# Feed-forward products of a 256-token, thirteen-stage network on one Trainium2 core: three moving products of 256 columns in place of one of 512 and one of 256

## The reference, cut to what matters

```python
def swiglu(x, w_in, w_out):
    gate, up = jnp.split(x @ w_in, 2, axis=-1)
    return (jax.nn.silu(gate) * up) @ w_out
...
x = x + 0.5 * swiglu(rms(x, gain), w_in, w_out)   # w_in: 1024 x 5632, w_out: 2816 x 1024
```

## Time and profile before

| what | value |
|---|---|
| median of 3 executions | 2190.56 us (2188.40 to 2193.27) |
| the profiled execution | 2188.89 us |
| its span, first to last instruction | 2187.1 us |
| granted TensorE clock, mean over the span | 0.996 |
| matmuls | 14203 |

### The profile page before, as it was taken

How to read it: one execution, slowest core, us unless ns; L and a number is a source line. 1 busy time by engine, 2 the same in 40 slices (tenths; PEclk the granted TensorE clock), 3 DMA queues, 4 the chain that set the end, 5 groups by cost and what they waited for, 6 DMA issues and landing times.

```text
span 2187.1 us, 39606 instructions
## 1 busy us (share of the span) xinstructions
PE 2141.0 (98%) x14203; PEld 1930.5 (88%) x14203; DVE 1600.6 (73%) x1903; ACT 1301.1 (59%) x1801; POOL 583.3 (27%) x450
## 2 busy tenths in 40 slices
PE   8999899999999999999999999999999999999998
PEld 7889888888888899999888888999888888888887
DVE  7875798886787676666887687654887688677874
ACT  5664776665665556665665466454665466456663
POOL 3421662441342000000342143000342144122430
PEclk9999999999999999999999999999999999999999
DMA  6665457665566555544566566544566556534662
GB/s 211 193 201 168 126 176 259 191 203 184 172 191 213 167 164 159 159 147 149 173 192 204 166 193 218 161 137 144 173 192 209 164 190 195 189 109 145 192 218 99
DMA packets 371157, 387.92 MB, mean 177 GB/s; under 512 B 11334, under 2 KB 366031, under 8 KB 371056
## 3 DMA queue, kind: packets, MB, share of 16 engines
q1 hardware_dynamic: 357104, 369.14, 53.7%
q10 hardware_dynamic: 13952, 17.41, 2.5%
HBM read 376.02 MB, written 10.49 MB: 177 GB/s over the span
## 4 chain that ended last, share of the span: by engine, by line
PE 87%; DVE 7%; ACT 4%; issue 1%; POOL 0%; DMA 0%; ACTq 0%; DVEq 0%
PE ps L818 43%; PE ps L819 23%; PE ps L772 3%; PE ps L773 3%; PE ps L774 3%; DVE wlo L1683 1%; DVE xg L1701 1%; PE ps L862 1%; ACT whi L1275 1%; PE ps L793 1%; PE ps L794 1%; PE ps L795 1%; PE ps L863 1%; PE ps L864 1%; PE ps L1003 1%
## 5 line engine op out<-in xcount | busy, mean ns | idle before, releaser
L1683 DVE TENSOR_TENSOR wlo<-raw,whi 128x1024 fp32r<-128x1024 f32 (+2 forms) x652 | 881.7, 1363 | 155.0 <-ACT whi L1275 154.0
L818 PE MATMUL ps<-xg,whi 128*128 128x512 f32 x2816 | 981.9, 392 | 3.7 <-DVE xg L1701 1.7
L1275 ACT ACTIVATE whi<-raw 128x1024 fp32r<-128x1024 f32 (+2 forms) x652 | 720.7, 1113 | 192.4 <-PE ps L819 130.4
L819 PE MATMUL ps<-xg,wlo 128*128 128x256 f32 x2816 | 794.6, 282 | 0.0
L818 PEld LDWEIGHTS ps<-xg,whi 128*128 128x128 f32 x2816 | 529.4, 188 | 117.9 <-DVE xg L1701 3.5
L819 PEld LDWEIGHTS ps<-xg,wlo 128*128 128x128 f32 x2816 | 532.9, 189 | 0.2
L818 PE MATMUL ps<-hT,whi 128*128 128x512 f32 x1408 | 488.5, 390 | 0.0
L819 PE MATMUL ps<-hT,wlo 128*128 128x256 f32 x1408 | 397.1, 282 | 0.0
L818 PEld LDWEIGHTS ps<-hT,whi 128*128 128x128 f32 x1408 | 264.3, 188 | 55.4
L819 PEld LDWEIGHTS ps<-hT,wlo 128*128 128x128 f32 x1408 | 266.1, 189 | 0.0
L2183 POOL TENSOR_TENSOR gate_r<-gate,r 128x512 f32<-128x512 f32 x88 | 189.6, 2154 | 286.7 <-DVE gate L1761 286.7
(11 more groups left out here) (276 smaller groups left out, 3003.3 us busy)
## 6 DMA issues: line engine op xcount, KB each, us to landing
raw<-in_ffn_w_in SPq DMA_DIRECT2D x352, 512.0 KB, 3.5
raw<-in_ffn_w_out SPq DMA_DIRECT2D x64, 768.0 KB, 4.8
raw<-in_ffn_w_out SPq DMA_DIRECT2D x64, 640.0 KB, 4.9
raw<-in_w_kv SPq DMA_DIRECT2D x48, 512.0 KB, 3.6
raw<-in_a_w_in SPq DMA_DIRECT2D x32, 512.0 KB, 4.2
raw<-in_b_w_q SPq DMA_DIRECT2D x24, 512.0 KB, 3.9
raw<-in_sb_w_qkv SPq DMA_DIRECT2D x24, 512.0 KB, 4.4
bias_by_distance<-bias_rows ACTq DMA_DIRECT2D x12, 768.0 KB, 5.4
```

The costliest lines, as they stand in the source:

```text
L818: nc.tensor.matmul(out, whi[:, par, w], both, start=first and k == 0, stop=False)
L819: mm = nc.tensor.matmul(out[:, 0:T], wlo[:, par, w], both[:, 0:T], start=False, stop=last and k == total - 1)
L1275: nc.scalar.activation(whi[:, par, off:off + size], raw[:, 2 * par + half, :size], ACT.Copy).then_inc(hi_done, 1)
L1683: nc.vector.tensor_tensor(wlo[:, par, off:off + size], raw[:, 2 * par + half, :size], whi[:, par, off:off + size].bitcast(F32), ALU.subtra ...
```

## The change

`wide_products` becomes `ffn_products`. For each chunk and half it issues three matmuls of 256 columns, all into the same 256 columns of one bank: half m of the slot is columns 256m to 256m+255. `start` is set on the slot's first matmul alone. The up slots use banks 4 and 0, the down slots banks 3 and 5. In "up" ACT's copy takes the whole sum (512 columns of one bank) and raises `evac_done` itself; the DVE additions of lines 1756 and 1768 are gone, with their semaphores. In "down" one DVE instruction in place of two adds half of the sum to `x`.

```diff
-    UP_BANKS, DOWN_BANKS = (3, 0), (3, 5)
+    UP_BANKS, DOWN_BANKS = (4, 0), (3, 5)
...
-                    both = moving[:, chunk0 + k, :, :].rearrange("p s t -> p (s t)")
+                    hi, lo = moving[:, chunk0 + k, 0, :], moving[:, chunk0 + k, 1, :]
                     for m in range(2):
-                        out = ps[:, bank + m, :]
+                        out = ps[:, bank, T * m:T * (m + 1)]
                         w = slice(W2 * k + P * m, W2 * k + P * (m + 1))
-                        nc.tensor.matmul(out, whi[:, par, w], both, start=first and k == 0, stop=False)
-                        mm = nc.tensor.matmul(out[:, 0:T], wlo[:, par, w], both[:, 0:T], start=False, stop=last and k == total - 1)
+                        nc.tensor.matmul(out, whi[:, par, w], hi, start=first and k == 0 and m == 0, stop=False)
+                        nc.tensor.matmul(out, whi[:, par, w], lo, start=False, stop=False)
+                        mm = nc.tensor.matmul(out, wlo[:, par, w], hi, start=False, stop=last and k == total - 1 and m == 1)
...
-                nc.scalar.activation(pair(gate[:, :]), wide(UP_BANKS[0], 0), ACT.Copy).then_inc(gate_copied, 1)
+                nc.scalar.activation(gate[:, :], ps[:, UP_BANKS[0], :], ACT.Copy).then_inc(evac_done, 1)
...
-                nc.scalar.activation(pair(h[:, :]), wide(UP_BANKS[1], 0), ACT.Copy).then_inc(h_copied, 1)
+                nc.scalar.activation(h[:, :], ps[:, UP_BANKS[1], :], ACT.Copy).then_inc(evac_done, 1)
...
-                dve.wait_ge(gate_copied, p + 1)
-                nc.vector.tensor_tensor(pair(gate[:, :]), wide(UP_BANKS[0], 1), pair(gate[:, :]), ALU.add).then_inc(evac_done, 1)
...
-                dve.wait_ge(h_copied, p + 1)
-                nc.vector.tensor_tensor(pair(h[:, :]), wide(UP_BANKS[1], 1), pair(h[:, :]), ALU.add).then_inc(evac_done, 1)
...
-                nc.vector.scalar_tensor_tensor(pair(xpair(m)), wide(DOWN_BANKS[m % 2], 1), 0.5, pair(xpair(m)), ALU.mult, ALU.add).then_inc(half_added, 1)
-                dve.wait_ge(half_added, NPAIR * f + m + 1)
-                nc.vector.scalar_tensor_tensor(pair(xpair(m)), wide(DOWN_BANKS[m % 2], 0), 0.5, pair(xpair(m)), ALU.mult, ALU.add).then_inc(evac_done, 1)
+                nc.vector.scalar_tensor_tensor(xpair(m), ps[:, DOWN_BANKS[m % 2], :], 0.5, xpair(m), ALU.mult, ALU.add).then_inc(evac_done, 1)
```

More of the change, by code:

```diff
@@ L343, in build_program @@
     r_col_ready = sem("r_col_ready")
-    gate_copied = sem("gate_copied")
-    h_copied, h_made = sem("h_copied"), sem("h_made")
+    h_made = sem("h_made")
     gate_made = sem("gate_made")
-    half_added = sem("half_added")
     gate_exp = sem("gate_exp")
@@ L393, in hidden @@
         return hT[:, bass.ds(2 * i, 2), part, :]
-    def wide(bank, part):
-        return ps[:, bank:bank + 2, T * part:T * (part + 1)]
     x_flat = flat(x[:, :, :])
@@ L801, in value_products, with ffn_products @@
             mm.then_inc(slot_done, 1)
-        def wide_products(n, n2, par, kind, moving, fill, bank, waits, first=True, last=True, chunk0=0, mid=None):
+        def ffn_products(n, n2, par, kind, moving, fill, bank, waits, first=True, last=True, chunk0=0, mid=None):
             if first:
@@ L838, in body @@
                     sums = waits and j == 1 and norms[f"up{f}"] != norms.get(before.get(f"up{f}"))
-                    wide_products(*at(st, i, j), "k8", xg, st["fill"] + j + 2 * i, UP_BANKS[j], waits,
+                    ffn_products(*at(st, i, j), "k8", xg, st["fill"] + j + 2 * i, UP_BANKS[j], waits,
                                   mid=(lambda: sum_squares(e)) if sums else None)
@@ L851, in ffn @@
                         waits = {max(k - k0, 0): w for k, w in needs.items()}
-                        wide_products(*at(st, 2 * i + m, j), "k11", hT, st["fill"] + m + 2 * i, DOWN_BANKS[m], waits,
+                        ffn_products(*at(st, 2 * i + m, j), "k11", hT, st["fill"] + m + 2 * i, DOWN_BANKS[m], waits,
                                       first=j == 0, last=j == 1, chunk0=FC // 2 * j)
```

## The result

| | before | after |
|---|---|---|
| median of the runs, us | 2190.43 | 2202.19 (2201.41 to 2203.28) |
| ratio, 95% interval | 1 | 1.005 (1.0037 to 1.0063) |
| profiled execution / its span, us | 2188.89 / 2187.1 | 2201.62 / 2199.8 |
| matmuls | 14203 | 18427 |

The changed kernel is 0.5% slower, which is more than the 0.2% that a measurement can tell. The forecast was +26.9 us, the runs show +11.8. The direction was right and the size was not: 2202.2 lies at the low edge of the range, and it is rival A's time (2204.2) and not the forecast's.

What follows compares the result with a forecast made beforehand. The prediction took TensorE's unbroken matmul stream as the bound. Its terms, +0.6 + 26.8 - 0.5 = +26.9 us on the profiled 2188.89, gave 2215.8, and 2217.5 us for the median, range 2202 to 2223.

Steps and rivals of the forecast that it cites:

- rival A: In the feed-forwards, the loop's waits or branches reset the phase, most triples beat at 0.350: 2204.2 us, chance 0.28.
- The bound: In "up" and "down" TensorE never idles, so a feed-forward lasts as long as its matmuls' beat.
- DVE's relief: Joining additions and 32 x updates leave DVE, some 143 us; worth nothing on the path where TensorE never idles.
- So I take 0.350 for the 24 and 0.3533 for the 504: Beats of a feed-forward's triples ahead of and behind sum_squares: +0.6 us and +26.8 us over eight feed-forwards.
- The three mixers of the earlier trace: Evidence for the slow beat: all three mixer stretches behind a sum_squares beat at 0.3533 us a triple.
- in all eight: Premise that sum_squares breaks the stream in the first round's second slot of all eight feed-forwards.
- Turns of the loop: Six instructions in place of four at the feed-forward loop's turns: taken as 0, from above 18 us.
- evac_done: Signal from ACT's copy, about one addition (0.69 us) earlier; TensorE waits for nothing there: 0.
- the new signals: At the feed-forward's evacuation nothing new is queued behind the signal, no wait or DMA added: 0.
- The third load: New weight load in each feed-forward triple, 4224 in all; said to lie inside the beats read from the mixers.
- The tail: At the kernel's end the last x update before the norm comes earlier, between 0 and 0.72 us: taken as -0.5.
- The rule of the Trainium skill: A matmul in a stream takes N/2.4 + 2.5 ns; estimated +10.6 us for the 4224 added feed-forward matmuls.

Runs made afterwards that it cites:

- E2: The kernel before, with its pairs, without the joining additions and with 32 of its 64 x updates left out: 2191.82 us, ratio 1.0002.
- E1: The changed kernel with the first slot of every feed-forward (16 weight tiles, ahead of sum_squares) back in pairs: 2208.64 us, ratio 1.0082 against the kernel before.
- E7: The changed kernel with the low-weight product cut into two matmuls of 128 columns, each with its own load: 2635.39 us, ratio 1.2041 against the kernel before.
- E10: The changed kernel with feed-forward matmuls at 128 columns in place of 256, in 3808 of 4224 tiles: profiled execution 2162.67 us, a second one 2323.64.
- E4: The changed kernel with pairs and their additions put back in "up", triples in "down" alone: 2194.18 us, ratio 1.0024 against the kernel before.

## Why the prediction was wrong in size

- **The bound was right.** TensorE without idle time in "up" and "down", before and after, clock at 1.00 (the 2.4 GHz level). DVE's relief, counted as 0, is 0 (E2, 1.0002). With the additions gone DVE is at 80.74 of 113.90 us (E2), not at 94 as the prediction has it.
- **The step that failed** is "So I take 0.350 for the 24 and 0.3533 for the 504", with its term of +26.8 us. The 504 beat at 0.3500, so that with the 24 the triples cost 4224 x 3.33 ns = 14.1 us; 14.3 were measured. I took sum_squares as what sets the phase. In these runs one of two beats followed it, according to the phase in which the stream reached it. The three mixers of the earlier trace rows were no independent cases: all three had come out of even steps, which the trace of before held for whoever looked at single steps instead of beats. It also held a fourth stretch of triples behind a sum_squares, which the prediction left out: that of the first mixer, behind two more small matmuls. Line 772 has 14 distances there over 4.9 us, 0.350 each:

```profile
L772 PE MATMUL ps<-xg,whi x15: 277/278/281, 206.3 to 211.2; 128*128 128x256 f32 x15
```

So it was three of four and not three of three. After the change the feed-forwards bring uneven steps to the same place.

- **Rival A** had the time and the beat, but its reason was off. It had waits and branches of the loop setting the phase anew. E1 holds 0.3533 over the same turns, so the turns leave the phase alone.
- **The premise "in all eight" was wrong.** sum_squares is in seven feed-forwards; the seventh shares its norm with the mixer ahead. By the forecast's own rule this would have been 504 x 3.3 ns = 1.7 us less.
- **Turns of the loop, evac_done and the new signals were counted as 0, and are 0.** The third load is a bound that I didn't price: I saw it only as lying "inside the beats". By E7 three loads take 339 of the 350 ns, so there is little room under this beat. Where the 3.3 ns above the pair come from stays open.
- **The tail** was taken as -0.5, between 0 and -0.72; it is -0.23 (E2 and after). Of the two updates of the earlier trace rows one is left, and DVE had been idle for 10.53 us ahead of it:

```profile
2190.02 0.69 DVE L1771 SCALAR_TENSOR_TENSOR x<-ps,x 128x512 f32<-128x512 f32 x1 [10.53 <-PE ps L815]
```

- **Not in the sum**: -0.5 us ahead of the first "up" and -0.8 in one mixer. That mixer took 166.05 to 170.10 us from kernel to kernel. In all of them short stretches at the clock's 1.2 GHz level (3.4, 6.8 and 3.4 us in before and after) fall in it, at places that shift; that they make the difference wasn't tested. The two make 1.3 of the 2.0 us by which the median lies under rival A's 2204.2; the rest is within the spread of the runs.
- **The rule of the Trainium skill** ("TensorE: Matmul & The Clock Gate", back-to-back issue gap), N/2.4 + 2.5 ns, made an estimated +10.6 us of the added matmuls. The section adds what the prediction left out, that the formula has no allowance for the weight loads of a real stream. 14.3 were measured, and its level (109 ns) is below the measured 116.7. It was nearer than my choice, and would be far off for E7, where it gives the same 2.5 ns against 102.6.

## What to carry to other kernels

When a stream of TensorE is the bound, price a change of its shape by the loads as well as by the columns. At full clock a matmul with its own load took 112 to 113 ns at the least, however few its columns (E7, E10), so narrower ones saved next to nothing, and of the forms tried here one wide matmul for each load was the cheapest. Here 512 + 256 columns cost 0.3467 us, three times 256 cost 0.3500 and 256 + 256 + 128 + 128 cost 0.453. Work taken off an engine that has cover (here 141 us of DVE) is worth nothing, and a beat read from other stages may hold only if the stream comes into them in the same phase: look at single steps, not only at the mean, and at every stretch that the trace has.

## What the runs showed of the hardware that was not expected

- The same three instructions have two steady beats, 0.3500 and 0.3533 us, set by what went ahead and kept for 500 tiles and more. Even steps ahead of sum_squares led to the slow one (23 of 23 in nine kernels, with one exception in E10), any other pattern to the fast one (39 of 39). Why is open.
- At the 1.2 GHz level a 128-column matmul with its own load takes about 213 ns (E10), at 2.4 GHz 111.7. The floor under narrow matmuls moves with the clock.
- An operation of DVE takes over twice as long beside one of POOL. The groups of after, by line and shape:

```profile
L1679 DVE TENSOR_TENSOR wlo<-raw,whi 128x1024 fp32r<-128x1024 f32 x524 | 720.6, 1384 | 135.1 <-ACT whi L1271 135.0
L1759 DVE TENSOR_SCALAR gate_e<-gate_e 128x512 f32<-128x512 f32 x88 | 74.0, 841 | 5.6 <-ACT gate_e L1313 5.6
L2173 POOL TENSOR_TENSOR gate_r<-gate,r 128x512 f32<-128x512 f32 x88 | 144.2, 1638 | 279.8 <-DVE gate L1755 279.8
```

and the same three of the kernel before:

```profile
L1683 DVE TENSOR_TENSOR wlo<-raw,whi 128x1024 fp32r<-128x1024 f32 x524 | 674.1, 1295 | 110.7 <-ACT whi L1275 110.4
L1765 DVE TENSOR_SCALAR gate_e<-gate_e 128x512 f32<-128x512 f32 x88 | 129.6, 1472 | 5.6 <-ACT gate_e L1317 5.6
L2183 POOL TENSOR_TENSOR gate_r<-gate,r 128x512 f32<-128x512 f32 x88 | 189.6, 2154 | 286.7 <-DVE gate L1761 286.7
```

Nobody changed these three operations, yet `gate_e` went from 1472 to 841 ns, `gate_r` from 2154 to 1638, and the splits from 1295 to 1384. E2 shows all three as well (854, 1647 and 1388 ns), E4, which keeps the additions of "up", doesn't (1473, 2153 and 1296). So it is the additions' going in "up" that shifts which of DVE's instructions run beside POOL's. Two rounds of after show what that does, the first with `gate_e` beside POOL's `gate_r`, the second with `gate_e` behind it:

```profile
400.24 2.21 POOL L2173 TENSOR_TENSOR gate_r<-gate,r 128x512 f32<-128x512 f32 x1 [1.76 <-DVE gate L1755]
401.21 1.51 DVE L1759 TENSOR_SCALAR gate_e<-gate_e 128x512 f32<-128x512 f32 x1
...
420.90 1.30 POOL L2173 TENSOR_TENSOR gate_r<-gate,r 128x512 f32<-128x512 f32 x1 [2.09 <-DVE gate L1755]
423.20 0.41 DVE L1759 TENSOR_SCALAR gate_e<-gate_e 128x512 f32<-128x512 f32 x1
```

In after 50 of the 88 `gate_e` overlap with no operation of POOL, and each of them takes 411 to 416 ns. The other 38 overlap with `gate_r` and take 959 to 1529 ns. In before all 88 overlap, and take 961 to 1532. `gate_r` takes 2204 to 2490 ns in the 30 rounds of after in which a split and `gate_e` both overlap with it, and 1292 to 1305 in the other 58. Why the splits got longer wasn't traced. Here it is all under cover.
